# First four levels of a blocked triangular inverse: doubling on TensorE, or substitution on VectorE through DRAM

## The reference, cut to what matters

```python
lmat = jnp.einsum("bhnid,bhnjd->bhnij", k_beta, k) * decay
rhs = jnp.concatenate([v_beta, k_beta * jnp.exp(g)[..., None]], axis=-1)
sol = lax.linalg.triangular_solve(lmat, rhs, left_side=True, lower=True, unit_diagonal=True)
```

## Time and profile before

| | us |
|---|---|
| median of 3 runs (1664.36 to 1665.73) | 1664.52 |
| the profiled execution, own time | 1663.31 |
| its span, first to last instruction | 1661.5 |
| TensorE matmul busy in the span | 1556.8 |
| VectorE busy | 534.6 |
| ScalarE busy | 351.2 |

### The profile page before, as it was taken

The page is one execution under the profiler, slowest core; times in us unless marked ns, Lnnn a source line. Parts: engine busy times, 40 slices in busy tenths (PEclk is TensorE's granted clock), DMA queues, the critical chain, the costliest instruction groups (busy, mean ns, idle before and its releaser), DMA issues.

```text
span 1661.5 us, 30306 instructions
## 1 busy us (share of the span) xinstructions
PE 1556.8 (94%) x13192; PEld 1320.8 (79%) x13192; DVE 534.6 (32%) x1286; ACT 351.2 (21%) x768; POOL 0.2 (0%) x4
## 2 busy tenths in 40 slices
PE   8999899999999999999999999998799988888798
PEld 7868788997888888888788888887677766676676
DVE  1444245321134440116762434013322222222222
ACT  1142212234010000101444531101111111111111
POOL 0000000000000000000000000000000000000000
PEclk9999999999999999999999999998799999999999
DMA  7332322122434433434223232465499999999993
GB/s 300 140 108 101 102 77 77 64 76 90 152 130 152 153 116 120 192 126 138 94 99 118 86 127 102 152 251 230 178 420 419 419 419 420 419 419 420 419 420 147
DMA packets 48659, 340.24 MB, mean 205 GB/s; under 512 B 5520, under 2 KB 6160, under 8 KB 9232
## 3 DMA queue, kind: packets, MB, share of 16 engines
q1 hardware_dynamic: 48528, 338.31, 52.5%
HBM read 406.45 MB, written 1.05 MB: 245 GB/s over the span
## 4 chain that ended last, share of the span: by engine, by line
PE 83%; DMA 8%; DVE 4%; issue 2%; ACT 1%; SPq 0%; DVEq 0%; ACTq 0%
PE bank L359 34%; PE bank L403 8%; PE bank L953 8%; DMA work<-w_gate_e_dram 6%; PE bank L373 6%; PE bank L973 4%; PE bank L984 3%; PE bank L997 3%; PE bank L419 2%; DMA ring<-w_gate_e_dram 2%; PE bank L497 2%; PE bank L624 1%; PE bank L335 1%; DVE work L1527 1%; PE bank L615 1%
## 5 line engine op out<-in xcount | busy, mean ns | idle before, releaser
L359 PE MATMUL bank<-hT,ring 128*128 128x256 f32 x2080 | 460.7, 383 | 9.7 <-DVE work L1521 6.3
L359 PEld LDWEIGHTS bank<-hT,ring 128*128 128x128 f32 x2080 | 396.5, 192 | 68.6 <-issue 16.1
L1530 DVE TENSOR_TENSOR xT<-xT,bank 128x512 f32<-128x512 f32 x100 | 68.8, 688 | 347.0 <-PE bank L973 226.4
L359 PE MATMUL bank<-work,ring 128*128 128x256 f32 x640 | 140.9, 382 | 0.0
L359 PEld LDWEIGHTS bank<-work,ring 128*128 128x128 f32 x640 | 122.6, 192 | 16.9 <-issue 0.5
L403 PE MATMUL bank<-work,ring 128*128 128x256 f32 x608 | 131.6, 379 | 0.0
L403 PEld LDWEIGHTS bank<-work,ring 128*128 128x128 f32 x608 | 115.8, 190 | 15.5
L953 PE MATMUL bank<-work 128*32 128x128 f32 x2240 | 100.8, 277 | 16.7 <-issue 9.7
L953 PEld LDWEIGHTS bank<-work 128*32 128x32 f32 x2240 | 92.4, 112 | 27.7 <-issue 27.7
L953 PE MATMUL bank<-ring,work 128*32 128x128 f32 x1728 | 99.1, 276 | 13.8 <-issue 10.0
L953 PEld LDWEIGHTS bank<-ring,work 128*32 128x32 f32 x1728 | 90.8, 111 | 22.9 <-issue 22.7
(11 more groups left out here) (305 smaller groups left out, 1724.0 us busy)
## 6 DMA issues: line engine op xcount, KB each, us to landing
work<-w_gate_e_dram SPq DMA_DIRECT2D x35, 1024.0 KB, 26.3
work<-w_up_e_dram SPq DMA_DIRECT2D x35, 1024.0 KB, 25.2
work<-w_down_e_dram SPq DMA_DIRECT2D x32, 1024.0 KB, 26.4
ring<-w_down_e_dram SPq DMA_DIRECT2D x27, 1024.0 KB, 26.0
ring<-w_gate_e_dram SPq DMA_DIRECT2D x25, 1024.0 KB, 26.0
ring<-w_up_e_dram SPq DMA_DIRECT2D x25, 1024.0 KB, 25.7
ring<-w_up_dram SPq DMA_DIRECT2D x22, 1024.0 KB, 4.9
hT<-w_gate_e_dram SPq DMA_DIRECT2D x22, 1024.0 KB
```

The source lines that it names most:

```text
L359: m = mm(b[:, j * SEQ:(j + 1) * SEQ], w[:, k, j * P:(j + 1) * P], tile(k), start=(k == 0), stop=(k == kt - 1))
L1530: return v.tensor_tensor(dst, a, b, ALU.add)
```

## The change

Levels 0 to 3 are removed on every engine. In their place the 16 x 16 diagonal blocks are inverted by substitution on VectorE, all at once: 16 problems with 8 diagonal blocks each are 128 blocks, one to a partition. For that the blocks are laid out anew through DRAM. Level 4 is then the first doubling level.

```diff
+SIDE, FIRST = 16, 4
+BLOCKS = P // SIDE
+        blk, inv, inv_t = (area(24064 + 256 * i, SIDE, SIDE) for i in range(3))
+        step_t = area(24832, SIDE, SIDE)
+        low_dram, inv_dram, inv_t_dram = (nc.dram_tensor(n, (BLOCKS, PROB, SIDE, SIDE), F32, kind="Internal").ap()
+                                          for n in ("low_blocks", "inverse_blocks", "inverse_blocks_t"))
```

TensorE makes `o_mla` 0 to 3, `vt` and `gates` 0 one after the other, then waits for the inverse, then runs levels 4 to 6 with `gates` 1 to 3 in them:

```diff
             to_features(("o_mla", 0), "w_o_mla", obT)
-            (level 0: four transposes of BT for each quad)
             to_features(("o_mla", 1), "w_o_mla", obT)
+            to_features(("o_mla", 2), "w_o_mla", obT)
+            (the vt transposes, moved here from behind level 2)
+            to_features(("o_mla", 3), "w_o_mla", obT)
+            to_features(("gates", 0), "w_gates", hT)
+            pe.wait_ge(S("inverse_landed"), 2 * 16 * BLOCKS)
-            for s in range(1, LEVELS):
+            for s in range(FIRST, LEVELS):
```

SyncE gets the transfers, inside the loop of weight loads, at the unit six behind `o_mla` 0 (that is `gates` 2):

```diff
+            def invert_blocks():
+                sp.wait_ge(S("lower_ready"), 1)
+                for b in range(BLOCKS):
+                    rows = slice(b * SIDE, (b + 1) * SIDE)
+                    sp.dma_start(low_dram[b].rearrange("p j i -> j p i"), LT[rows, :, rows]).then_inc(S("lower_out"), 16)
+                sp.wait_ge(S("lower_out"), 16 * BLOCKS)
+                sp.dma_start(blk[:, :, :], low_dram.rearrange("b p j i -> (b p) j i")).then_inc(S("blocks_landed"), 16)
+                sp.wait_ge(S("blocks_inverted"), 1)
+                sp.dma_start(inv_dram.rearrange("b p i n -> (b p) i n"), inv[:, :, :]).then_inc(S("inverse_out"), 16)
+                sp.dma_start(inv_t_dram.rearrange("b p n i -> (b p) n i"), inv_t[:, :, :]).then_inc(S("inverse_out"), 16)
+                sp.wait_ge(S("inverse_out"), 32)
+                sp.wait_ge(S("inverse_cleared"), 2)
+                for b in range(BLOCKS):
+                    rows = slice(b * SIDE, (b + 1) * SIDE)
+                    sp.dma_start(T[rows, :, rows], inv_dram[b].rearrange("p i n -> i p n")).then_inc(S("inverse_landed"), 16)
+                    sp.dma_start(TTr[rows, :, rows], inv_t_dram[b].rearrange("p n i -> n p i")).then_inc(S("inverse_landed"), 16)
             for u, (name, i, n) in enumerate(UNITS):
                 if u >= RING:
                     sp.wait_ge(product_ready, unit_product[u - RING] + 1)
+                if u == UNITS.index(("w_o_mla", 0, 2048)) + RING:
+                    invert_blocks()
                 sp.dma_start(ring[u % RING][:, 0:n], A[name][i]).then_inc(landed[u % RING], 16)
```

VectorE clears `inv` after the last `LT` and `AT` are written (and raises `lower_ready` by that), and runs the substitution after `gated_mla(0)`:

```diff
+                if q == 3:
+                    dve.wait_ge(bank_free("qk", 3), used("qk", 3))
+                    v.memset(inv[:, :, :], 0.0).then_inc(S("lower_ready"), 1)
                 conv_qkv(8 + q)
...
             gated_mla(0)
+            v.memset(inv[:, :, :].rearrange("p a b -> p (a b)")[:, 0:SIDE * SIDE:SIDE + 1], 1.0).then_inc(S("dve_step"), 1)
+            dve.wait_ge(S("blocks_landed"), 16)
+            for j in range(SIDE - 1):
+                n, w = SIDE - 1 - j, j + 1
+                mul(step_t[:, 0:n, 0:w], b3(blk[:, j, j + 1:SIDE], n, w), rep(inv[:, j, 0:w], n, w)).then_inc(S("dve_step"), 1)
+                dve.wait_ge(S("dve_step"), nth("dve_step"))
+                tt(inv[:, j + 1:SIDE, 0:w], inv[:, j + 1:SIDE, 0:w], step_t[:, 0:n, 0:w], ALU.subtract).then_inc(S("dve_step"), 1)
+                dve.wait_ge(S("dve_step"), nth("dve_step"))
+            v.tensor_copy(inv_t[:, :, :], inv[:, :, :].rearrange("p i n -> p n i")).then_inc(S("blocks_inverted"), 1)
+            gated_mla(1)
+            gated_mla(2)
+            (the four beta products of vt, moved here from level 3)
+            gated_mla(3)
```

More of the change, by code:

```diff
@@ L596, in _ @@
             to_features(("o_mla", 0), "w_o_mla", obT)
[L597 to L603, removed]
-            to_features(("o_mla", 1), "w_o_mla", obT)
-            for s in range(1, LEVELS):
+            to_features(("o_mla", 1), "w_o_mla", obT)
+            to_features(("o_mla", 2), "w_o_mla", obT)
+            for i in range(8, 12):
+                pe.wait_ge(bank_free("qkv", i), used("qkv", i))
+            pe.wait_ge(S("v_ready"), 1)
+            for c in range(TT):
+                for hq in range(2):
+                    b = new("vt", c * 2 + hq)
+                    pe.wait_ge(bank_free("vt", c * 2 + hq), used("vt", c * 2 + hq) - 1)
+                    for p in range(4):
+                        m = nc.tensor.transpose(b[:, p * P:(p + 1) * P],
+                                                qkvT[:, 16 + hq * 4 + p, c * P:(c + 1) * P], ident)
+                    m.then_inc(product_ready, 1)
+            to_features(("o_mla", 3), "w_o_mla", obT)
+            to_features(("gates", 0), "w_gates", hT)
+            pe.wait_ge(S("inverse_landed"), 2 * 16 * BLOCKS)
+            for s in range(FIRST, LEVELS):
                 def bt_t(q):
                     pe.wait_ge(S("off_diagonal"), nth("off_diagonal"))
-                    if s == 1:
-                        pe.wait_ge(bank_free("Y", 0, q), used("Y", 0, q))
-                    else:
+                    if s > FIRST:
                         pe.wait_ge(bank_free("TT", s - 1, q), used("TT", s - 1, q))
@@ L647, in _ @@
                 turn_t(1)
[L648 to L651, removed]
+                to_features(("gates", s - 3), "w_gates", hT)
                 turn_t(2)
                 turn_t(3)
[L654 to L665, removed]
             for q in range(4):
@@ L1084, in _ @@
             sp.wait_ge(S("stored"), 16)
+        @block.gpsimd
+        def _(pool):
+            flat = lambda a: a[:, :, :].rearrange("p h i -> p (h i)")
+            pool.wait_ge(product_ready, made("mla_o", HEADS - 1))
+            nc.gpsimd.memset(flat(TTr), 0.0).then_inc(S("inverse_cleared"), 1)
+            pool.wait_ge(S("lower_ready"), 1)
+            nc.gpsimd.memset(flat(T), 0.0).then_inc(S("inverse_cleared"), 1)
         @block.scalar
@@ L1262, in _ @@
             A_(flat(gB), flat(gB), ACT.Sigmoid).then_inc(S("gB_ready"), 1)
-            for s in range(1, LEVELS):
+            gate_kept(0)
+            for s in range(FIRST, LEVELS):
                 def t_kept(q):
@@ L1270, in _ @@
                 for q in range(4):
-                    if q >= 2 or s > 1:
+                    if q >= 2 or s > FIRST:
                         act.wait_ge(product_ready, made(("YT", s, q - 2) if q >= 2 else ("YT", s - 1, q + 2)))
@@ L1277, in _ @@
                 t_kept(1)
-                if s >= 3:
-                    gate_kept(s - 3)
+                gate_kept(s - 3)
                 t_kept(2)
@@ L1729, in off_diagonal @@
                     .then_inc(S("off_diagonal"), 1)
[L1731 to L1745, removed]
             def gated_mla(i):
@@ L1754, in _ @@
             gated_mla(0)
-            for s_ in range(1, LEVELS):
+            dve.wait_ge(S("lower_ready"), 1)
+            v.memset(inv[:, :, :].rearrange("p a b -> p (a b)")[:, 0:SIDE * SIDE:SIDE + 1], 1.0).then_inc(S("dve_step"), 1)
[6 more added lines that the diff above has]
+                tt(inv[:, j + 1:SIDE, 0:w], inv[:, j + 1:SIDE, 0:w], step_t[:, 0:n, 0:w], ALU.subtract).then_inc(S("dve_step"), 1)
+                dve.wait_ge(S("dve_step"), nth("dve_step"))
+            v.tensor_copy(inv_t[:, :, :], inv[:, :, :].rearrange("p i n -> p n i")).then_inc(S("blocks_inverted"), 1)
+            gated_mla(1)
+            gated_mla(2)
+            dve.wait_ge(product_ready, made("vt", 3))
+            for n in range(4):
+                key = ("vt", n)
+                mul(vb[:, n * 4:n * 4 + 4, :], quads(at(key)[:, :]), b3(beta[:, n * 4:n * 4 + 4], 4, P)).then_inc(bank_free(key), 1)
+            gated_mla(3)
+            for s_ in range(FIRST, LEVELS):
                 for q in range(4):
-                    dve.wait_ge(product_ready, made(("Y", s_, q - 2) if q >= 2 else ("Y", s_ - 1, q + 2)))
+                    if q >= 2 or s_ > FIRST:
+                        dve.wait_ge(product_ready, made(("Y", s_, q - 2) if q >= 2 else ("Y", s_ - 1, q + 2)))
                     off_diagonal(s_, q)
[L1759 to L1765, removed]
                 for q in range(4):
@@ L1769, in _ @@
                     dve.wait_ge(product_ready, made(k))
+                    dve.wait_ge(S("inverse_landed"), 2 * 16 * BLOCKS)
                     tt(TTr[:, four, :], TTr[:, four, :], quads(at(k)[:, :]), ALU.subtract).then_inc(bank_free(k), 1)
```

## The result

| | before | after |
|---|---|---|
| median, us (4 runs each) | 1664.44 (1661.36 to 1665.73) | 1627.21 (1625.62 to 1628.52) |
| the profiled execution, own time | 1663.31 | 1625.62 |
| its span | 1661.5 | 1623.5 |
| start of level 4 in the span | 314.36 | 278.23 |

The change is faster by 37.2 us; the ratio of the runs is 0.9775, 95% interval 0.9758 to 0.9792. The direction was forecast, and so was the time that the removed levels give back.

What follows compares the result with a forecast made beforehand. TensorE, busy 94% of the span, was taken as the bound. Profiled 1663.31 less 33.2 (35.8 gained, less a 2.6 wait for a chain of 32.0) gave 1630.1; plus 1.2 for the median, 1631.3 us, range 1627.5 to 1647.

Steps and rivals of the forecast that it cites:

- What goes: Between `o_mla` 0 and level 4, removing levels 0 to 3 starts level 4 at 278.60, 35.8 us earlier, if TensorE never waits.
- the wait of 2.6: Before level 4, TensorE ready at 278.6 waits 2.6 us for the inverse, landing at 281.2; gain 33.2.
- eight stores of blocks: Eight DMAs out of `LT` in 64-byte runs: seven issues at 0.58 and a landing of 2.6, 6.7 us.
- steps and copy: VectorE's substitution of 30 dependent steps, 7.35 us, and the turned copy, 0.35: 7.7 us.
- two stores: Stores of the inverse after the substitution: one issue of 0.58 and a landing of 2.6, 3.2 us.
- sixteen loads: Last phase of the chain, 256 runs of 64 bytes each: 15 issues at 0.58 plus 2.6, 11.3 us.
- hand-overs: Five semaphore hand-overs between engines along the chain, 0.1 us each: 0.5 us.
- Rival A: At level 4 no wait at all, issues at 0.33, chain 26.2 us: 1628.7 us; chance 0.50 together with the forecast.
- the cover of 29.4: TensorE's work from 249.20 to level 4, four units and the `vt` transposes, 29.40 us, beside which the chain runs.
- The low end of the range: For the whole kernel's time, 1627.5 us, set a little under the 1628.7 of no wait at all.
- Descriptors: In the 64-byte transfers issuing sets the pace, not moving; a run costs at most 0.060 us, kept for the range.
- Rival C: In the two strided phases 64-byte runs are paid one by one per queue, 0.174 us each: slower, 1685.3 us; chance 0.10.

Runs made afterwards that it cites:

- side32late: The changed kernel with blocks of side 32 and `gates` 1 made before TensorE's wait, transfers still started behind `o_mla` 0: 1622.95 us, ratio 0.975 to the kernel before.
- fill0: The kernel before with `o_mla` 1 moved between the second and third quad of level 0: 1662.97 us, ratio 0.9994.
- elem: The changed kernel with the contiguous store of the turned inverse replaced by sixteen stores in runs of 4 bytes: 1685.08 us, ratio 1.0124 to the kernel before.
- early: The changed kernel with the chain's transfers started before the wait for `o_mla` 0 instead of behind it: 1626.11 us, ratio 0.9773 to the kernel before.
- twice: The changed kernel with the substitution run twice over the same blocks: 1634.20 us, ratio 0.9827 to the kernel before.
- side32: The changed kernel with blocks of side 32, level 5 first, transfers started earlier, `gates` 1 before TensorE's wait: 1618.15 us, ratio 0.9724 to the kernel before.

## Why the prediction was wrong, by its own steps

**What goes** was right. TensorE does four units and the transposes in the time given. Level 4 starts 0.37 ahead of the 278.60 worked out, which is the 0.35 that this execution was ahead at `o_mla` 0, and 35.8 of gain at that point stands against 35.8. The beta products were hidden as said, VectorE's 30 steps and copy took 263.62 - 255.96 = 7.66 against 7.7, level 4 itself did not change (330.28 - 314.36 = 15.92 before, 294.09 - 278.23 = 15.86 after), and nothing after 360 us gave the gain back.

**The step that failed is the size of the transfers in the chain**, with it the wait of 2.6, and with it the forecast:

| term | predicted | measured |
|---|---|---|
| eight stores of blocks | 6.7 | 253.90 - 248.89 = 5.0 |
| load of `blk` | 2.6 | 2.06 |
| steps and copy | 7.7 | 7.66 |
| two stores | 3.2 | 267.35 - 263.62 = 3.7 |
| sixteen loads | 11.3 | 276.6 - 267.35 = 9.2 |
| hand-overs | 0.5 | within the others |
| sum | 32.0 | 27.7 |

The price of an issue was taken at the middle of its bounds, 0.58, because the patterns are less regular. They cost 0.45 and 0.04 between them, 0.49 from start to start, and over the 22 steps of the two phases that is 2.2 less. The landing was taken from a small transfer issued behind another at the start of the kernel, 2.6; these landed in 1.7 to 2.0 (128 KB of `blk` in 2.06 with the hand-over), another 2.0 less. The hand-overs take no room of their own, 0.5 less, and the two stores took 0.5 more. Together, but for rounding, that is the difference of 4.3: the false wait of 2.6 and the spare time of 1.6 that stands in its place.

Rival A, counted within the forecast at 50%, had the outcome: no wait, and 1628.7. Its terms were not right either. It priced the issues at 0.33, where they cost 0.49, and the landings at 2.6, and the two errors nearly cancel (26.2 against 27.7). Both sums are under the cover of 29.4, so its outcome did not depend on that.

The forecast also charged no slow clock for its wait of 2.6, since both stalls in the rows were longer. The wait did not occur, but later runs had stops near that length: 2.9 us in `side32late` was followed by a unit at clock 0.81, 2.2 in `fill0` by products at 0.64. So that term at nothing was not safe.

**The low end of the range** is a second, smaller error. It left 1.2 under A, and the time is 1.5 under A. Nothing in it allowed for how far executions of one kernel differ: the fastest and the slowest run of a kernel lie 1.3 to 7.9 apart in this document, and `o_mla` 0 alone starts anywhere in a span of 2.6. The prediction used only for stretches after a stall that it could name. The interval of the ratio allows a gain between 34.6 and 40.3, so the measured 37.2 doesn't show that the change is worth more than the 35.8 of its profile.

**Descriptors.** The low price was right, 10.4 ns, almost six times under the 0.060 us of the earlier trace rows. The Trainium skill, "DMA: Bandwidth & Descriptors", section Bandwidth, puts a floor of 0.67 us at 4 KB, for loads that GpSimd issues, down to 64 packets at about 10.5 ns, which is a price counted over the whole transfer. So taken, the sixteen loads would need an estimated 43 us, and they took 9.2: the trace does not agree. The same number comes out only per engine, where 16 work side by side and 4096 runs are 256 x 10.4 ns = 2.7 us; the page does not say that, and that the two numbers are alike may be chance. Rival C was rightly held small for 64-byte runs, and the 4-byte store shows that its mechanism is real.

**The rest.** GpSimd's clears took 1.80 each; the one of `TTr` ran from 194.96 on and delayed nothing (TensorE waits 5.92 for VectorE there, and 5.93 in before). `gates` 2 was loaded 20 us ahead of its need.

## What to carry to other kernels

Work moved off the engine that bounds was free here exactly as long as it landed before that engine got there: work out both arrival times, and treat the difference as a budget to be spent (here on one level more). Beyond it each microsecond costs itself, and after a stall a slow group. Price the transfers of such a chain from the nearest rows, each with its issue and its landing, for they were 20 of the 27.7 us: runs of 64 bytes were hidden behind their issues, runs of 4 bytes were not. When an engine takes on a long sequence, look at which banks its queued copies hold. And when two waits follow each other, charge the one that ends last: the stop for the bank in `side32late` cost nothing, since the inverse was later still.

## What the runs showed of the hardware

- A transfer of 256 runs of 64 bytes cost SyncE 0.45 us to issue (0.49 from start to start), a plain 1 MB load 0.33. It landed in 1.7 us as a store and in 1.9 to 2.0 as a load (medians, profile of the change).
- A 64-byte packet occupied its DMA engine for 10.4 ns in the sixteen loads. In `elem` sixteen stores of 2048 runs of 4 bytes filled all queues for 59.7 us, 29 ns a run.
- Two stores of 128 KB, one behind the other, took 3.7 us in the profile of the change and 2.2 in those of `early` and `twice`.
- VectorE's two-operand steps in float32 took 0.19 us at 15 elements and 0.22 at 64 on 128 partitions, and 0.42 at 256 on 64 partitions, with 0.03 between dependent ones.
- After a stop of 4.4 us (`twice`) TensorE's first group took 3.47 for 1.78, at granted clock 0.56; after one of 2.9 (`side32late`) a unit took 8.83 for 7.07, at 0.81; after one of 1.4 (`side32`) the first group took 2.05 for 1.78, at 1.00.
